# Attention layer: two index projections interleaved, weights rounded by halves, index weights copied out first

## The reference, cut to what matters

```python
h = rms_norm(x, norm_g[l]) * (1.0 + scale[:, None, :]) + shift[:, None, :]
z = h @ odd_w_in[j]
q, k, v, qi, ki, wi, g = split_cols(z, ODD_SIZES)
qi = rope(qi.reshape(B, S, IDX_HEADS, IDX_HEAD_DIM), positions)
ki = rope(ki[:, :, None, :], positions)[:, :, 0, :]
...
idx_logits = jnp.einsum('bqhd,bsd->bqhs', qib, kf) * (IDX_HEAD_DIM ** -0.5)
score = jnp.einsum('bqh,bqhs->bqs', wib * (IDX_HEADS ** -0.5), jax.nn.relu(idx_logits))
top_val, top_idx = lax.top_k(score, k_sel)
```

## Time and profile before

| what | value |
|---|---|
| runs, device us | 1795.55, 1795.36, 1793.77; median 1795.36 |
| profiled execution | 1796.12 us, its span 1794.4 us, mean granted clock 0.988 |
| busy: PE, DVE, ACT, POOL | 95%, 70%, 45%, 46% of the span |
| odd layer's ki and qi0 blocks | from 751.9 to 767.5 us of the span |
| index scores and picks | from 776.3 to about 925 us |

### The profile page before, as it was taken

The page is one execution under the profiler, slowest core; times in us unless marked ns, Lnnn a source line. Parts: engine busy times, 40 slices in busy tenths (PEclk is TensorE's granted clock), DMA queues, the critical chain, the costliest instruction groups (busy, mean ns, idle before and its releaser), DMA issues. The chain is left out here.

```text
span 1794.4 us, 32762 instructions
## 1 busy us (share of the span) xinstructions
PE 1713.4 (95%) x13216; PEld 1281.4 (71%) x13216; DVE 1256.2 (70%) x2279; ACT 801.2 (45%) x1498; POOL 829.3 (46%) x726
## 2 busy tenths in 40 slices
PE   5899999999999999999999999999999999999997
PEld 5677777777777668767766666587777777777766
DVE  7599999999999696369975655534888517255553
ACT  3444444434533363364434434434676533344442
POOL 3544344344443275377851111544555555544433
PEclk9999999999999999899999999999999999999998
DMA  7212322222222132222221111122322232333312
GB/s 299 94 61 76 103 69 76 96 78 67 95 92 88 48 127 97 76 71 71 88 77 36 36 36 36 35 95 86 102 73 83 71 103 75 138 118 121 112 53 92
DMA packets 51877, 154.73 MB, mean 86 GB/s; under 512 B 5888, under 2 KB 12032, under 8 KB 51600
## 3 DMA queue, kind: packets, MB, share of 16 engines
q1 hardware_dynamic: 51728, 152.65, 25.3%
HBM read 150.50 MB, written 2.13 MB: 85 GB/s over the span
## 5 line engine op out<-in xcount | busy, mean ns | idle before, releaser
L487 POOL TENSOR_TENSOR w_lo<-raw,w_hi 128x512 fp32r<-128x512 f32 (+2 forms) x434 | 584.9, 1368 | 645.8 <-ACT w_hi L469 645.4
L513 PE MATMUL bank<-h_hi,w_hi 128*128 128x512 f32 x1368 | 585.7, 428 | 15.4 <-DVE attn_tmp L2389 4.0
L517 PE MATMUL bank<-h_lo,w_hi 128*128 128x512 f32 x1368 | 542.9, 397 | 7.5 <-DVE h_lo L933 5.0
L514 PE MATMUL bank<-h_hi,w_lo 128*128 128x512 f32 x1368 | 539.8, 395 | 0.0
L469 ACT ACTIVATE w_hi<-raw 128x512 fp32r<-128x512 f32 (+2 forms) x434 | 241.7, 601 | 272.9 <-PE bank L517 191.1
L513 PEld LDWEIGHTS bank<-h_hi,w_hi 128*128 128x128 f32 x1368 | 260.6, 191 | 103.0 <-issue 45.2
L517 PEld LDWEIGHTS bank<-h_lo,w_hi 128*128 128x128 f32 x1368 | 259.6, 190 | 74.7 <-DVE h_lo L933 9.7
L514 PEld LDWEIGHTS bank<-h_hi,w_lo 128*128 128x128 f32 x1368 | 261.2, 191 | 59.7 <-issue 13.7
L1569 DVE SCALAR_TENSOR_TENSOR ya<-padded,vecs,ya 128x512 f32<-128x512 f32 x240 | 216.1, 901 | 3.9
L2359 ACT ACTIVATE probs<-probs,small 128x512 f32<-128x512 f32 x64 | 46.3, 723 | 107.0 <-DVE small L2342 106.8
L3062 DVE CUSTOM_DVE_ANT_0 fox_probs<-bank,fox_keybias 128x128 f32<-128x128 f32 (+3 forms) x64 | 28.8, 488 | 84.6 <-PE bank L2986 84.3
(11 more groups left out here) (396 smaller groups left out, 2779.1 us busy)
## 6 DMA issues: line engine op xcount, KB each, us to landing
raw<-even_in SPq DMA_DIRECT2D x57, 512.0 KB, 3.9
raw<-odd_in SPq DMA_DIRECT2D x39, 512.0 KB, 3.5
raw<-ada SPq DMA_DIRECT2D x32, 512.0 KB, 4.2
raw<-fox_in SPq DMA_DIRECT2D x25, 512.0 KB, 3.7
raw<-lru_in SPq DMA_DIRECT2D x24, 512.0 KB, 3.4
ada_first<-ada SPq DMA_DIRECT2D x16, 512.0 KB, 14.4
raw<-even_out SPq DMA_DIRECT2D x16, 512.0 KB, 3.5
raw<-odd_out SPq DMA_DIRECT2D x16, 512.0 KB, 3.5
```

The lines of the kernel that those rows point to most:

```text
L487: e.tensor_tensor(k.w_lo[s % NSPLIT][:, at], k.raw[n % NRAW][:, at], k.w_hi[s % NSPLIT][:, at].bitcast(F32), ALU.subtract).then_inc(*did(" ...
L513: e.matmul(out, hi[:, w], x[i][0], start=start and i == 0, stop=False, skip_group_check=True)
L514: e.matmul(out, lo[:, w], x[i][0], start=False, stop=False, skip_group_check=True)
L517: m = e.matmul(out, hi[:, w], x[i][1], start=False, stop=stop and i == kt - 1, skip_group_check=True)
```

## The change

Four edits. (1) ki and qi0 are two streams in PE's merge, so their steps alternate: ki's step i, then qi0's step i. Both end together, and what reads ki comes at -3.1 in place of -4.01. (2) The first half of a block's weights, everywhere in the program where sizes fit, waits only until the block two before is half projected; so the matmul of step 3 of each block signals. (3) The halves of qi1's weights are placed by hand on ACT and POOL: the first before the end of ki, the second after. (4) ACT copies the index weights (`wi`) out before it does anything else with ki's bank; before, this came last.

```diff
@@ half_block
-    return n, key, slice(half * size, (half + 1) * size), k.plan[k.split[s - NSPLIT]][0] if s >= NSPLIT else None
+    old = None
+    if s >= NSPLIT:
+        old_key, _, old_kt, old_width, _ = k.plan[k.split[s - NSPLIT]]
+        soon = half == 0 and size <= old_kt // 2 * old_width
+        old = ("projected", old_key, old_kt // 2 - 1) if soon else ("projected", old_key)
+    return n, key, slice(half * size, (half + 1) * size), old
@@ project
-        elif key in LEAVING:
+        elif key in LEAVING or i == kt // 2 - 1:
             m.then_inc(*did("projected", key, i))
@@ main_times, main_end
+    if key in INDEX[:2]:
+        return [block_number(INDEX[0]) + (2 * i + 0.5 + INDEX.index(key)) / DT for i in range(DT)]
+def main_end(key):
+    return block_number(key) + (1.9 if key == INDEX[0] else 0.99)
@@ odd_tensor
-    merge(main(), index_weights(), turn_values(), scores())
+    merge(main(INDEX[:1]), main(INDEX[1:] + MAIN), index_weights(), turn_values(), scores())
@@ odd_scalar, main
+            if key == INDEX[0]:
+                yield at - 0.7
+                round_half(k, e, need, did, k.nth[key] + NSPLIT, 0)
+                yield at
+                ready(("projected", key))
+                e.activation(k.turning[2][0:IH, :], k.bank.get(key, k.banks[0])[64:64 + IH, :], ACT.Copy).then_inc(
+                    *did("activated", "wi"))
+                round_half(k, e, need, did, k.nth[key] + NSPLIT, 1)
...
-            if key[0] == "ki":
-                e.activation(k.turning[2][0:IH, :], k.bank.get(key, k.banks[0])[64:64 + IH, :], ACT.Copy).then_inc(
-                    *did("activated", "wi"))
@@ odd_gpsimd, main
+            if key == INDEX[0]:
+                for half in range(2):
+                    yield main_end(key) - 0.7 * (1 - half)
+                    rest_half(k, e, need, did, k.nth[key] + NSPLIT, half)
```

More of the change, by code:

```diff
@@ L466, in round_half @@
     n, key, at, old = half_block(k, s, half)
-    for w in need((f"raw{n % NRAW}", key), old and ("projected", old)):
+    for w in need((f"raw{n % NRAW}", key), old):
         e.wait_ge(*w)
@@ L484, in rest_half @@
     n, key, at, old = half_block(k, s, half)
-    for w in need(("rounded", key, half), old and ("projected", old), (f"raw{n % NRAW}", key)):
+    for w in need(("rounded", key, half), old, (f"raw{n % NRAW}", key)):
         e.wait_ge(*w)
@@ L560, in project_values @@
                 m = e.matmul(bank[:, :], k.H[ch][1][:, at], hi[:, w], start=False, stop=ch == DT - 1, skip_group_check=True)
-        m.then_inc(*did("projected", key))
+            m.then_inc(*(did("projected", key) if i == kt - 1 else did("projected", key, i)))
 def start_gpsimd(k, e):
@@ L2252, in scores, with main @@
                      skip_group_check=True).then_inc(*did("multiplied", "score", i))
-    def main():
-        for key in INDEX + MAIN:
+    def main(keys):
+        for key in keys:
             at = main_times(key)
@@ L2432, in main @@
         for key in INDEX + MAIN:
-            at = block_number(key) + 0.99
+            at = main_end(key)
             if key[0] == "g":
@@ L2591, in main @@
         for key in INDEX + MAIN:
-            yield block_number(key) + 0.99
+            if key == INDEX[0]:
+                for half in range(2):
+                    yield main_end(key) - 0.7 * (1 - half)
+                    rest_half(k, e, need, did, k.nth[key] + NSPLIT, half)
+            yield main_end(key)
             if key[0] in ("v", "g"):
```

## The result

The changed kernel took **1798.97 us** (median of 14 runs, 1796.29 to 1801.65), the kernel before 1795.61 beside it (14 runs, 1791.95 to 1796.99): a ratio of **1.0023, 95% interval 1.0016 to 1.0030**. On 1795.61 that is 4.1 us more, between 2.9 and 5.4. The forecast was +2.3 us. The time lies in its range, but past its middle: a small loss that can be told from no change. The prediction gave 0.17 to a time over 1798.9.

What follows compares the result with a forecast made beforehand. TensorE was taken as the bound, busy 1713.4 of 1794.4 us. Bank wait net of interleave +1.2, clock +1.5, earlier halves -0.4 gave +2.3 us, 1797.7 us; range 1793.6 to 1800.2, the forecast's own 1796.5 to 1798.9.

Steps and rivals of the forecast that it cites:

- The interleave's own gain: In the ki and qi0 pair: the interleaved matmuls run without gaps and end at 765.6 us, 1.8 us gained.
- The wait that takes its place: Before qi1: PE stands 4.0 us until ki's bank is emptied; the first score comes 1.2 us later.
- The clock: Right behind the gap before qi1: a low clock for 3.2 us costs 1.5 us, bounds nothing and 3.0 us.
- Rival 1: Behind the gap before qi1: bank wait but clock kept, +0.8 us, 1796.2 us; chance 0.20.
- Rival 2: Behind the gap before qi1: clock low for longer, 6.4 us, giving +3.8 us, 1799.2 us; chance 0.16.
- Earlier first halves, elsewhere: In the first pair of heads: a shorter wait for ACT wins 0.4 us; bounds nothing and 4.3 us.
- The sum: Whole kernel: +1.2 + 1.5 - 0.4 = +2.3 us, so 1797.7 us against 1795.36.

Runs made afterwards that it cites:

- no_halves: The changed kernel with the earlier first halves taken back everywhere but for qi1's weights; 1800.02 us, ratio 1.0021 to the kernel before.
- filler: The changed kernel with 16 matmuls into an unused bank put in the gap before qi1; 1797.55 us, ratio 1.0004 to the kernel before.
- third_bank: The changed kernel with ki's bank taken from the other ring, the five work banks; 1797.54 us, ratio 1.0012 to the kernel before.
- interleave_only: The kernel before with the interleave alone, index weights copied last and no halves moved; 1799.23 us, ratio 1.0021 to the kernel before.
- halves_only: The kernel before with the earlier first halves of the blocks' weights and nothing else; 1795.21 us, ratio 1.0003 to the kernel before.
- late_halves: stagger_bank with the earlier first halves in blocks 49 to 54 alone, the even layer's last heads; 1794.89 us, ratio 0.9996 to the kernel before.
- sequence: The changed kernel with the interleave alone taken back, ki's eight steps before qi0's eight; 1795.89 us, ratio 1.0007 to the kernel before.
- early_halves: stagger_bank with the earlier first halves in the first 49 blocks alone; 1790.88 us, ratio 0.9974 to the kernel before.
- stagger: no_halves with the interleave shifted: ki's first five steps alone, qi0's steps 0 to 2 between ki's last three; 1792.28 us, ratio 0.9985 to the kernel before.
- stagger_bank: stagger with ki's bank taken from the other ring; 1791.72 us, ratio 0.9984 to the kernel before.

## Why the prediction was right or wrong

**The interleave's own gain (1.8 us): right.** The pair ran without gaps. From ki's start to the turn of the index weights it took 15.54 us before and 13.45, 13.88 and 14.04 in changed, no_halves and filler: 1.5 to 2.1 us gained.

**The wait that takes its place: right, to a few tenths.** Index weights at 765.08 (forecast 765.3), swap of ki from 766.21 (766.5), qi1 at 770.22 (770.35), gap 4.09 us (4.0), first scores at 778.80 without a wait for POOL (near 779). Its price without the clock was put at 1.2 us; the three traces give 0.6 to 1.2. That the bank is the wait was only half of it: third_bank has no bank wait and still no gain, since ki's late end delays the turned qi0 by itself. The rule of the Trainium skill that was cited there ("Perfetto Trace Analysis", "Matmuls": groups of matmuls go round the banks) pointed at the right place, and the gap agrees with it; but another bank was not the cure, ending ki earlier was.

**The clock (1.5 us, bounds 0 and 3.0): right, and the spread is real.** The lower level came in all three traces with the gap (4.09, 4.10 and, in interleave_only, 3.66 us). It cost 1.6 us (changed) and 2.1 us (no_halves) against filler. Rival 1, clock kept, did not occur. Rival 2's stretch, twice 3.2 us, occurred in no_halves with the same gap, but a third of it lay in the gap, so that it cost 2.1 us and not 3.0.

**Earlier first halves, elsewhere (-0.4 us): the step that failed.** It took edit 2 "at nothing, with at most tenths for more waits", with nothing as its lower bound, so that a loss was left out. The gain at 57 us is there in the size forecast where the clock holds at 47, and near 0.2 us in the changed kernel's own trace. The cost is in the even layer's last heads: +0.5 us at the first new wait and 1.1 at the second where the clock holds there. In the changed kernel's trace the last heads take 121.79 us in place of 120.17. With the clock down near 588 they take 122.9 (halves_only, third_bank) in place of 121.7; there the second wait is gone, and 0.5 to 0.6 of these 1.2 us are the pause of unknown cause. late_halves and sequence reach 123.3 and filler 125.4, with a longer pause or a further low clock. Without those the term is thus +0.7 us (1.2 less the full gain of 0.5) to +1.6 (no gain), and +1.4 in the changed kernel's own trace, instead of -0.4. The runs as wholes show it less clearly: halves_only stands at +0.5 us (-1.1 to +2.2), changed and no_halves cannot be told apart, and only early_halves and late_halves differ beyond their intervals.

**The sum.** Pair +2.2 (here) to +3.1 (no_halves), halves +0.7 to +1.6: +2.9 to +4.7 us, against 4.1 measured, 2.9 to 5.4. With +1.1 for the halves the forecast's own sum would have been 3.8 us, 1799.2. That the time lies in the range is in part luck: its upper end was drawn from rival 2, a longer low clock, and not from this cost, and the pair came out at +2.2 us where +2.7 was forecast. In the profiled execution the 3.7 us of the span are the pair's 2.2, the last heads' 1.6, 0.3 between the first scores and PE's wait near 874, and three more: -0.7 before 545 us and -0.6 in the norm ahead of ki, which other traces show too without a pattern by the edits, and +0.9 at the lru layer's gates. There the load of the weights took 7.4 us from its issue, before 6.5. Only halves_only (7.2 us) and late_halves (7.8) wait there too, for 0.7 and 1.35 us; whether the moved halves have a part in it is open.

## What to carry to other kernels

Before two blocks are made to end together, count the readers of the first: their time must lie under the second block's matmuls, or on a ring of two the block after next stands, and with a spare bank the work behind the readers is late all the same. Interleave so that the block with the longest chain of readers still ends first; that turned +3.8 us (no_halves) into -2.7 (stagger). And an edit that lets off-path engines work earlier everywhere is not free where they share time with an engine that PE waits for: give it a loss in the bounds, and apply it only where a row shows the wait that it removes (early_halves has the lowest ratio, 0.26% under before, though its interval overlaps stagger_bank's).

## What the runs showed of the hardware

The granted clock differs between executions behind the very same gaps. In the even layer's last heads PE is busy for 2.17 of the 4 us before 588, in both of the kernels below; the one kept the clock, the other did not. The kernel before:

```profile
584.00:588.00 4.00, 2.17 (x83) 1.78 (x86) 1.83 (x4) 1.69 (x4) 2.03 (x2) 1.00 0.00 0
588.00:592.00 4.00, 4.00 (x50) 3.38 (x42) 3.86 (x5) 1.46 (x4) 1.22 (x2) 1.00 0.38 134
```

and stagger, whose program is the same in that layer but for signals:

```profile
584.00:588.00 4.00, 2.17 (x69) 1.73 (x69) 2.55 (x4) 1.69 (x4) 2.50 (x2) 0.91 0.00 0
588.00:592.00 4.00, 4.00 (x14) 3.37 (x15) 3.86 (x6) 0.64 (x2) 0.00 (x0) 0.66 0.40 135
```

It costs 121.70 - 120.17 = 1.5 us, and six of the twelve traces had it: four of the six with the last heads' halves moved, two of the six without. Likewise the gap of 4.1 us cost 1.6 or 2.1 us. Such throws are as large as most terms of this study, so a stretch of a trace is best compared with several traces of the same stretch, up clock with up clock, before a difference is put down to an edit.
